# A seven-product block scheme in fp32 projections: the third and fourth weight sums become one vector operation, and the sums' rounding and remainder one operation each

## The reference, cut to what matters

```python
h = h + jnp.concatenate([o_gdn, o_moba], axis=-1) @ w_o[i]
hn = rms_norm(h, ffn_norm[i])
h = h + (jax.nn.silu(hn @ w_gate[i]) * (hn @ w_up[i])) @ w_down[i]
gate = jax.nn.sigmoid(rms_norm(h, ple_norm[i]) @ w_ple_gate[i])
h = h + gate * (p[i] @ w_ple_proj[i])
```

## Time and profile before

| | |
|---|---|
| median of 3 runs | 1308.66 us |
| span of the profiled execution, first to last instruction | 1306.8 us |
| TensorE busy (matmuls) | 1299.9 us, 99% |
| VectorE busy | 1041.3 us, 80% |
| ScalarE busy | 710.7 us, 54% |
| GpSimd busy | 57.2 us, 4% |
| TensorE's granted clock over the span | 1.000 of 2.4 GHz |

### The profile page before, as it was taken

The page is one execution under the profiler, slowest core; times in us unless marked ns, Lnnn a source line. Parts: engine busy times, 40 slices in busy tenths (PEclk is TensorE's granted clock), DMA queues, the critical chain, the costliest instruction groups (busy, mean ns, idle before and its releaser), DMA issues.

```text
span 1306.8 us, 18407 instructions
## 1 busy us (share of the span) xinstructions
PE 1299.9 (99%) x6589; PEld 1074.1 (82%) x6589; DVE 1041.3 (80%) x1409; ACT 710.7 (54%) x946; POOL 57.2 (4%) x71
## 2 busy tenths in 40 slices
PE   9999999999999999999999999999999999999998
PEld 8788888888888888888888888888888888888887
DVE  6578885788586668999888978679888987968784
ACT  6576444544455556655555654445555555555653
POOL 5003000221000000000000000000000000000000
PEclk9999999999999999999999999999999999999999
DMA  8555554455444555665566656566666566556554
GB/s 272 178 176 162 160 147 129 146 147 148 145 127 145 178 176 161 215 219 181 188 198 205 204 187 215 182 211 188 195 205 214 181 189 210 190 178 224 178 179 163
DMA packets 126204, 238.37 MB, mean 182 GB/s; under 512 B 9711, under 2 KB 10786, under 8 KB 126138
## 3 DMA queue, kind: packets, MB, share of 16 engines
q1 hardware_dynamic: 126106, 237.48, 58.2%
q10 hardware_dynamic: 32, 0.01, 0.0%
HBM read 235.36 MB, written 2.10 MB: 182 GB/s over the span
## 4 chain that ended last, share of the span: by engine, by line
PE 97%; DVE 2%; ACT 0%; DMA 0%; issue 0%; DVEq 0%; ACTq 0%
PE pair L654 15%; PE pair L656 15%; PE pair L655 15%; PE pair L935 12%; PE pair L937 12%; PE pair L936 12%; PE bg L935 2%; PE bg L936 2%; PE bg L937 2%; PE bg L775 2%; PE bg L845 2%; PE bg L712 1%; PE bg L930 1%; DVE w_lo L1583 1%; PE bg L826 0%; PE bg L687 0%
## 5 line engine op out<-in xcount | busy, mean ns | idle before, releaser
L1583 DVE TENSOR_TENSOR w_lo<-raw,w_hi 128x1024 fp32r<-128x1024 f32 x442 | 533.1, 1222 | 160.7 <-ACT w_hi L1163 158.8
L1163 ACT ACTIVATE w_hi<-raw 128x1024 fp32r<-128x1024 f32 x399 | 416.4, 1056 | 254.6 <-PE pair L656 117.0
L654 PE MATMUL pair<-w_hi,xT_hi 128*128 128x512 f32 x716 | 289.7, 405 | 0.0
L656 PE MATMUL pair<-w_hi,xT_lo 128*128 128x512 f32 x716 | 279.9, 391 | 0.0
L655 PE MATMUL pair<-w_lo,xT_hi 128*128 128x512 f32 x716 | 279.4, 390 | 0.0
L656 PEld LDWEIGHTS pair<-w_hi,xT_lo 128*128 128x128 f32 x716 | 134.5, 188 | 29.1
L654 PEld LDWEIGHTS pair<-w_hi,xT_hi 128*128 128x128 f32 x716 | 134.7, 188 | 26.7 <-DVE w_lo L1583 0.3
L655 PEld LDWEIGHTS pair<-w_lo,xT_hi 128*128 128x128 f32 x716 | 134.9, 188 | 24.7
L1444 ACT ACTIVATE w_hi<-raw 128x1024 fp32r<-128x1024 f32 x43 | 45.7, 1063 | 141.5 <-DVE raw L1915 140.0
L935 PE MATMUL pair<-w_hi,actT_hi 128*128 128x512 f32 x296 | 115.7, 391 | 0.0
L937 PE MATMUL pair<-w_hi,actT_lo 128*128 128x512 f32 x296 | 115.2, 389 | 0.0
(11 more groups left out here) (386 smaller groups left out, 1959.8 us busy)
## 6 DMA issues: line engine op xcount, KB each, us to landing
raw<-in_w_in_dram SPq DMA_DIRECT2D x112, 512.0 KB, 3.8
raw<-in_w_gate_dram SPq DMA_DIRECT2D x88, 512.0 KB, 4.4
raw<-in_w_up_dram SPq DMA_DIRECT2D x88, 512.0 KB, 4.4
raw<-in_w_down_dram SPq DMA_DIRECT2D x88, 512.0 KB, 4.8
raw<-in_w_o_dram SPq DMA_DIRECT2D x32, 512.0 KB, 4.4
raw<-in_w_ple_gate_dram SPq DMA_DIRECT2D x32, 512.0 KB, 4.8
raw<-in_w_ple_proj_dram SPq DMA_DIRECT2D x4, 512.0 KB, 4.3
h<-in_x_dram SPq DMA_DIRECT2D x3, 512.0 KB, 7.8
```

The lines of the kernel that those rows point to most:

```text
L654: mm(banks[t][:], hi[:, ts], wh, start=first, stop=False)
L656: m = mm(banks[t][:], lo[:, ts], wh, start=False, stop=last)
L1163: f(w_hi[j % RING][:], raw[j % RING][:], ACT.Copy).then_inc(hi_ready, 1)
L1583: v.tensor_tensor(w_lo[j % RING][:], raw[j % RING][:], w_hi[j % RING][:].bitcast(F32), ALU.subtract).then_inc(lo_ready, 1)
```

## The change

The signs of the scheme are turned. `t1 = u0 + g0` replaces the difference, `t2 = u1 - t1` stays, and then `t3 = g0 + t2` and `t4 = g1 + t2` are one operation of 128x1024 whose second operand is `t2`, read twice (a broadcast over the middle dimension). All three sums lie in one buffer `t_raw` of 128x1536. ScalarE rounds all three in one operation after it has waited for that sum, and behind the `between` step; VectorE forms all three remainders in one operation, waiting for this rounding. TensorE waits once, ahead of the product that takes `t3`. SyncE's wait moves from `t4_ready` to `t34_ready`. Where products are summed, two additions become subtractions per block. Some small constants move so that `t_raw` may lie over 6 KiB of tables that are no longer needed.

```diff
 # ScalarE, split_mixed
                 f(w_hi[j % RING][:], raw[j % RING][:], ACT.Copy).then_inc(hi_ready, 1)
+                if between:
+                    between()
                 if not n0_first:
                     act.wait_ge(t_used, n - 1)
-                f(t_hi[:, 2, :], t3_raw[:], ACT.Copy).then_inc(t3_hi_ready, 1)
-                if between:
-                    between()
-                act.wait_ge(t4_ready, n)
-                f(t_hi[:, 0:2, :], t24_raw[:], ACT.Copy).then_inc(t24_hi_ready, 1)
+                act.wait_ge(t34_ready, n)
+                f(t_hi[:], t_raw[:], ACT.Copy).then_inc(t_hi_ready, 1)
 # VectorE, split_mixed
-                v.tensor_tensor(t3_raw[:], raw[ju][:, 1, :], raw[ju][:, 0, :], ALU.subtract).then_inc(t3_ready, 1)
-                dve.wait_ge(t3_ready, n)
-                v.tensor_tensor(raw[ju][:, 0, :], raw[ju][:, 0, :], raw[jg][:, 0, :], ALU.subtract).then_inc(t1_ready, 1)
+                v.tensor_tensor(raw[ju][:, 0, :], raw[ju][:, 0, :], raw[jg][:, 0, :], ALU.add).then_inc(t1_ready, 1)
                 dve.wait_ge(t1_ready, n)
-                v.tensor_tensor(t24_raw[:, 0, :], raw[ju][:, 1, :], raw[ju][:, 0, :], ALU.subtract).then_inc(t2_ready, 1)
+                v.tensor_tensor(t_raw[:, 0, :], raw[ju][:, 1, :], raw[ju][:, 0, :], ALU.subtract).then_inc(t2_ready, 1)
                 dve.wait_ge(t2_ready, n)
-                v.tensor_tensor(t24_raw[:, 1, :], raw[jg][:, 1, :], t24_raw[:, 0, :], ALU.subtract).then_inc(t4_ready, 1)
+                v.tensor_tensor(t_raw[:, 1:3, :], raw[jg][:], t_raw[:, 0:1, :].to_broadcast([P, 2, CB]),
+                                ALU.add).then_inc(t34_ready, 1)
                 split(u, j)
                 if between:
                     between()
-                dve.wait_ge(t3_hi_ready, n)
-                v.tensor_tensor(t_lo[:, 2, :], t3_raw[:], t_hi[:, 2, :].bitcast(F32), ALU.subtract).then_inc(t3_lo_ready, 1)
-                dve.wait_ge(t24_hi_ready, n)
-                v.tensor_tensor(t_lo[:, 0:2, :], t24_raw[:], t_hi[:, 0:2, :].bitcast(F32),
-                                ALU.subtract).then_inc(t24_lo_ready, 1)
+                dve.wait_ge(t_hi_ready, n)
+                v.tensor_tensor(t_lo[:], t_raw[:], t_hi[:].bitcast(F32), ALU.subtract).then_inc(t_lo_ready, 1)
 # TensorE, mixed_units (and alike in down and in the last projection)
-                pe.wait_ge(t3_lo_ready, n)
-                product(bg[2][:], F_hi[:, q, 2, :], F_lo[:, q, 2, :], t_hi[:, 2, :], t_lo[:, 2, :], first, last)
-                pe.wait_ge(t24_lo_ready, n)
+                pe.wait_ge(t_lo_ready, n)
+                product(bg[2][:], F_hi[:, q, 2, :], F_lo[:, q, 2, :], t_hi[:, 1, :], t_lo[:, 1, :], first, last)
                 product(bg[1][:], F_hi[:, q, 0, :], F_lo[:, q, 0, :], t_hi[:, 0, :], t_lo[:, 0, :], first, last)
 # SyncE, three places
-                            sp.wait_ge(t4_ready, ...)
+                            sp.wait_ge(t34_ready, ...)
```

More of the change, by code:

```diff
@@ L295, in build @@
         u_s = sb("u_s", [P, CB], at=mix + 60 * KIB)
-        t3_raw = sb("t3_raw", [P, CB], at=mix + 62 * KIB)
         d_raw = sb("d_raw", [P, 2, P], at=mix + 62 * KIB)
@@ L311, in build @@
         triu_at = place[0]
-        t24_raw = sb("t24_raw", [P, 2, CB], at=triu_at)
+        t_raw = sb("t_raw", [P, 3, CB], at=triu_at)
         triu = sb("triu", [P, P])
@@ L329, in build @@
         exp_a = sb("exp_a", [P, HEADS])
-        sc = {n: sb(n, [P, NT, HEADS]) for n in ("beta", "dt_in", "dt_abs", "dt_exp", "dt_ln", "dt_sum", "g", "gc", "egc")}
         ba_s = sb("ba_s", [P, NT, 2 * HEADS])
         ba_parts = sb("ba_parts", [P, NT, 4 * HEADS])
+        assert triu_at + 6 * KIB <= place[0]
+        gains = sb("gains", [P, NROW + 2])
+        G_ATTN, G_FFN, G_PLE, G_GDN, G_Q, G_K = 0, KT, 2 * KT, 3 * KT, 3 * KT + 1, 3 * KT + 2
+        G_QS, G_OG = NROW, NROW + 1
+        sc = {n: sb(n, [P, NT, HEADS]) for n in ("beta", "dt_in", "dt_abs", "dt_exp", "dt_ln", "dt_sum", "g", "gc", "egc")}
         warm = sb("warm", [P, 1])
@@ L387, in build @@
             sem(n) for n in ("d_ready", "d_rounded", "xg_ready", "form_ready", "form_rounded"))
-        t1_ready, t2_ready, t3_ready, t4_ready = (sem(f"t{n}_ready") for n in (1, 2, 3, 4))
-        t3_hi_ready, t24_hi_ready, t3_lo_ready, t24_lo_ready, t_used = (
-            sem(n) for n in ("t3_hi_ready", "t24_hi_ready", "t3_lo_ready", "t24_lo_ready", "t_used"))
+        t1_ready, t2_ready, t34_ready = (sem(f"t{n}_ready") for n in (1, 2, 34))
+        t_hi_ready, t_lo_ready, t_used = (sem(n) for n in ("t_hi_ready", "t_lo_ready", "t_used"))
         p1_copied, gate_sum, v_ready, up_sum = (
@@ L1047, in down @@
                                     False).then_inc(unit_used, 1)
-                            pe.wait_ge(t3_lo_ready, count)
-                            product(bg[2][:], D_hi[:, q, 2, :], D_lo[:, q, 2, :], t_hi[:, 2, :], t_lo[:, 2, :], first, last)
-                            pe.wait_ge(t24_lo_ready, count)
+                            pe.wait_ge(t_lo_ready, count)
+                            product(bg[2][:], D_hi[:, q, 2, :], D_lo[:, q, 2, :], t_hi[:, 1, :], t_lo[:, 1, :], first, last)
                             product(bg[1][:], D_hi[:, q, 0, :], D_lo[:, q, 0, :], t_hi[:, 0, :], t_lo[:, 0, :], first, last)
-                            product(pair[0][1][:], actT_hi[:, k1, a1], actT_lo[:, k1, a1], t_hi[:, 1, :], t_lo[:, 1, :], False,
+                            product(pair[0][1][:], actT_hi[:, k1, a1], actT_lo[:, k1, a1], t_hi[:, 2, :], t_lo[:, 2, :], False,
                                     last).then_inc(t_used, 1)
@@ L1108, in _ @@
                             False).then_inc(unit_used, 1)
-                    pe.wait_ge(t3_lo_ready, MIX_PG + q + 1)
-                    product(bg[2][:], E_hi[:, q, 3, :], E_lo[:, q, 3, :], t_hi[:, 2, :], t_lo[:, 2, :], first, last)
-                    pe.wait_ge(t24_lo_ready, MIX_PG + q + 1)
+                    pe.wait_ge(t_lo_ready, MIX_PG + q + 1)
+                    product(bg[2][:], E_hi[:, q, 3, :], E_lo[:, q, 3, :], t_hi[:, 1, :], t_lo[:, 1, :], first, last)
                     product(bg[1][:], E_hi[:, q, 1, :], E_lo[:, q, 1, :], t_hi[:, 0, :], t_lo[:, 0, :], first, last)
-                    product(pair[0][1][:], xT_hi[:, k1, a1], xT_lo[:, k1, a1], t_hi[:, 1, :], t_lo[:, 1, :], False,
+                    product(pair[0][1][:], xT_hi[:, k1, a1], xT_lo[:, k1, a1], t_hi[:, 2, :], t_lo[:, 2, :], False,
                             last).then_inc(t_used, 1)
@@ L1950, in turned_forms, with add @@
                                 ALU.subtract).then_inc(ff_free[q], 1)
-            def add(o, a, b, done, count=None):
+            def add(o, a, b, done, count=None, op=ALU.add):
                 if count:
                     dve.wait_ge(down_sum, count)
-                v.tensor_tensor(o, a, b, ALU.add).then_inc(done, 1)
+                v.tensor_tensor(o, a, b, op).then_inc(done, 1)
             def down(ud, n, n0, m0):
@@ L1980, in down @@
                         add(o00, o00, pair[0][0][:], pair_free[0], d0 + 1)
-                        add(v_s[:], bg[1][:], v_s[:], down_sum)
+                        add(v_s[:], bg[1][:], v_s[:], down_sum, op=ALU.subtract)
                         add(u_s[:], bg[2][:], v_s[:], down_sum, d0 + 2)
                     if jj == end + 1:
-                        add(o10, o10, u_s[:], down_sum, d0 + 3)
+                        add(o10, o10, u_s[:], down_sum, d0 + 3, op=ALU.subtract)
                         add(o10, o10, pair[0][1][:], pair_free[0], d0 + 4)
@@ L2017, in gate_up @@
                         dve.wait_ge(p1_copied, i + (n0 + (2 if n0 else 0) + 1))
-                        v.tensor_tensor(v_s[:], bg[1][:], p1[:], ALU.add).then_inc(v_ready, 1)
+                        v.tensor_tensor(v_s[:], bg[1][:], p1[:], ALU.subtract).then_inc(v_ready, 1)
                         v.tensor_tensor(gate_s[0][:], pair[0][0][:], p1[:], ALU.add).then_inc(gate_sum, 1)
@@ L2022, in gate_up @@
                         dve.wait_ge(v_ready, i * 2 + (2 * n0 + 2))
-                        v.tensor_tensor(gate_s[1][:], pair[0][1][:], u_s[:], ALU.add).then_inc(gate_sum, 1)
+                        v.tensor_tensor(gate_s[1][:], pair[0][1][:], u_s[:], ALU.subtract).then_inc(gate_sum, 1)
                     if j == 2 * UPB - 1:
@@ L2067, in _ @@
                     dve.wait_ge(p1_copied, done + 4 + 1)
-                    v.tensor_tensor(v_s[:], bg[1][:], act_s[1][:], ALU.add).then_inc(v_ready, 1)
+                    v.tensor_tensor(v_s[:], bg[1][:], act_s[1][:], ALU.subtract).then_inc(v_ready, 1)
                     v.tensor_tensor(gate_s[0][:], pair[0][0][:], act_s[1][:], ALU.add).then_inc(gate_sum, 1)
```

12 lines of the change are left out of this document (4 added, 8 removed).

## The result

| | before | after |
|---|---|---|
| median | 1308.76 us (4 runs) | 1317.16 us (1316.73 to 1317.52, 4 runs) |
| ratio to before | | 1.0064, 95% interval 1.005 to 1.0078 |
| span of the profiled execution | 1306.8 us | 1315.0 us |
| VectorE busy | 1041.3 us | 1035.2 us |
| ScalarE busy | 710.7 us | 709.8 us |

The change makes the kernel 8.4 us slower. VectorE does 6.1 us less work and ScalarE 0.9 us less; the span is 8.2 us longer. The forecast was 1313.4 us with a range up to 1316.5. Its mechanism and its twelve places are in the trace; its sizes were too small.

What follows compares the result with a forecast made beforehand. TensorE, busy 1299.9 of 1306.8 us, was taken to bound the kernel. Losses of 3.15 (nine iterations), 1.0 (first block) and 0.57 us (down block) summed to 4.7: 1308.66 + 4.7 = 1313.4 us, range 1309.0 to 1316.5.

Steps and rivals of the forecast that it cites:

- the old stalls: TensorE's two waits for a second unit's remainder, 0.9 us listed, about 1.4 us with restarts: all the change can gain.
- the added wait: VectorE, done with `split` at about s + 3.8, waits for the joint rounding until s + 4.18; each mixed unit ends 0.22 later.
- no carry: Rival, 17%: room between an iteration's mixed units leaves the third only 0.22 us late, in time by 0.07; 1310.0 us.
- Grouping pays: Rival, 8%: the joint rounding ends by the time VectorE finishes `split`, each mixed unit 0.27 us shorter; 1307.3 us.
- the broadcast is slow: Rival, 6%: the joint sum takes 1.45 us, each mixed unit another 0.23 later, 0.69 by the third; 1320 us.
- the half of the rule that was taken: Skill's second half: where an engine isn't saturated but causes bubbles on another, breaking instructions up may let work finish sooner.
- the term for the nine iterations: Third mixed unit's remainder ends at 614.79, TensorE resumes at 614.95, not 614.60: 0.35 us lost, nine times, 3.15 us.
- The handover from VectorE's sums to the rounding: ScalarE starts the joint rounding 0.04 us after VectorE's sums, so it runs from s + 2.70 to s + 4.18.
- The `between` step: In an iteration's first mixed unit ScalarE's copies start at 593.92, 0.11 us earlier; the next `split` starts 0.20 later.
- The durations: Joint sum 1.22 us on VectorE, joint rounding 1.475 us on ScalarE, joint remainder 1.75 us on VectorE.
- The first block: Delays of 0.22 us per mixed unit add up; TensorE loses 0.78 by the second, 1.01 by the third: 1.0 us.
- the down block: Second stage's first down block: remainder ends 0.22 us later, TensorE runs at 1120.53, not 1119.96: 0.57 us lost.

Runs made afterwards that it cites:

- the best version: Changed kernel with rounding and remainder each in two operations, and TensorE taking the second sum's product first, behind that remainder alone: 1307.99 us, ratio 0.9994.
- the second: Changed kernel with its third and fourth sums as two operations of 128x512 again, rounding and remainder still joint: 1322.17 us, ratio 1.0101.
- the fourth experiment: Changed kernel with joint sum, rounding and remainder only in each gate-and-up block's third mixed unit; others four separate sums, rest in two operations: 1310.48 us, ratio 1.0012.
- the first experiment: Changed kernel with ScalarE's two waits ahead of the joint rounding in the other order, first for the sums: 1315.93 us, ratio 1.0053.

## Why the prediction was right and wrong

**Right: what bounds, and the bound on the gain.** In the kernel before, TensorE's pace holds the time, and the best version's median is 0.9 us under the kernel before, of the 1.4 that the old stalls allowed.

**Right: the added wait and who stands behind it.** VectorE's idle time ahead of the joint remainder was forecast at 0.4 us in most of 43 units; it is 0.47 in all. About twelve waits of TensorE were forecast at 0.2 to 0.7 us; there are twelve, at the places named. That the delays add within a block is shown by the second and the fourth experiment, and the "no carry" rival falls with them. It also falls by its own sign: the second unit of an iteration starts 0.33 us late (9.68 against 9.35 behind the first), where less than 0.1 would have spoken for it. "Grouping pays" falls with the 20.1 us of waits, "the broadcast is slow" with 1.226 us.

**Right: the half of the rule that was taken.** The Trainium skill's advice to break instructions up where an engine is not saturated but delays another ("Perfetto Trace Analysis", "Optimizing Scalar/DVE Operations") agrees with these runs: with the rounding in two operations 1308.86 us, with one 1317.16.

**Wrong: the size of the term for the nine iterations**, 0.35 us each in the forecast, 0.71 measured. This is the step that failed; the mechanism held. It is 3.2 of the 3.5 us by which the spans differ from the sum. The third unit's remainder was to be 0.64 us late against its old place; it is late by 616.98 - 614.15 = 2.83, less the 1.85 that TensorE had lost up to this iteration: 0.98. Three pieces of the working were short:

- *The handover from VectorE's sums to the rounding.* I took 0.04 us from the row of the second unit's rounding. Two waits stand ahead of that one as well, but the late one, for the sum, is written first there and last ahead of the joint rounding, which starts 0.09 behind the sums. That is 0.05 us more than I took in the second and again in the third unit, 0.11 by the end. Shown by the first experiment: with the waits in the other order 1.2 us of the 3.5 go.
- *The `between` step.* I had ScalarE's copies start 0.11 us earlier, on a handover of 0.04 from TensorE's transposes. They start at the same distance from the unit's first operation as before, 3.02 us (595.90 - 592.88; before 594.03 - 591.01), 0.15 behind the first four transposes in both kernels (593.28 + 0.60 = 593.88 to 594.03; 595.15 + 0.60 = 595.75 to 595.90). So do eight of the nine iterations before and all nine after. The row of before already held this wait: its copies showed no idle time, since the engine had been busy until then, and I read that as being bound by the rounding. 0.11 us per iteration, 1.0 us in all. TensorE's and ScalarE's rows in the changed kernel:

```profile
595.15 0.60 PE L928 MATMUL bg<-ident,act_s 128*128 128x128 f32 x4
...
595.90 1.09 ACT L1432 ACTIVATE actT_hi<-bg 128x512 f32 x2 [1.16 <-PE bg L928]
```

- *The durations* were each short by a little: 1.490 us for 1.475, 1.759 for 1.752, 1.226 for 1.22, 0.03 a unit, 0.09 by the third, 0.8 us over the nine.

Together 0.31 of the 0.34 us by which the third unit's remainder is later than forecast (0.98 against 0.64). The second and the third piece rest on the rows alone; no run undid them.

The first block (1.0 forecast, 1.15 measured) and the down block (0.57 and 0.7) were short in the same direction; in the down block it is about the 0.09 of its one unit.

**Wrong: the range.** It allowed 0.07 us per mixed unit for the handover as an outer case. The handover alone used up 0.05 of that, and the two other pieces were in the sum without a bound. Where a term is a small difference (0.64 late, less 0.45 of slack, plus 0.16 of restart) and is taken nine times over three links, an error of 0.1 us a link is 2.7 us. The range should have been worked out from such an error as well; added to the outer case of 1315.8 it reaches 1318.5.

## What to carry to other kernels

Joining two operations saves a fixed cost (a rounding of 128x1536 took 1.490 us, two of 128x512 and 128x1024 took 0.615 + 1.045), here on an engine with time to spare, and makes the first result wait for the last input. Ask of each join whether the engine that does it would stand idle while an early input lies ready, and who waits for the result. Here the joint remainder cost nothing, since VectorE had other work until its last input was there. The joint rounding cost 8 us: in the third unit the second sum was there at 612.34, ScalarE was free from 612.71, and it stood idle until 613.70. Where several such steps stand in one engine's queue ahead of a wait of the bounding engine, add up their delays over the queue before comparing them with the slack, and work the range out from an error per link.

## What the runs showed of the hardware that I had not expected

Two waits ahead of one ScalarE instruction do not cost the same in either order. In the changed kernel the one written last, for the sums (L1444), is an instruction of its own that runs 42 times on ScalarE's sequencer; with the two in the other order, L1444 is the line of the wait for TensorE's last use, and that one is the instruction of its own. The changed kernel, then the first experiment:

```profile
L1444 ACTq EVENT_SEMAPHORE  x42: 17/17/17, 521.7 to 1251.5; - x42
...
L1444 ACTq EVENT_SEMAPHORE  x38: 17/17/17, 520.1 to 1248.3; - x38
```

The Trainium skill states that instructions which wait for several engines may have such EventSemaphore instructions put ahead of them ("Perfetto Trace Analysis", "Identifying Dependency Chains"). The trace agrees, and adds the price: the rounding starts 0.09 us behind the sums with the late wait there, 0.03 with the early one there and the late one on the rounding itself. And ScalarE's copies behind TensorE's transposes start 0.15 us after them, where a step of the sequencer (`ACTq L1432`, 0.07 us in the chain above) lies between.
